# Nine input-projection blocks computed as seven block products during the first three attentions

## The reference

```python
proj = h @ w_in[layer]
(glu_a, glu_b, z_conv, q, k, v, z_att, g_conv, g_att) = jnp.split(proj, split_idx, axis=-1)
u = glu_a * jax.nn.sigmoid(glu_b)          # then a causal depthwise convolution of 31 taps
...                                         # silu(z_att) and sigmoid(g_conv), sigmoid(g_att) are used later
```

## Time and profile before

| | us |
|---|---|
| median of 3 runs (2577.93 to 2579.3) | 2578.81 |
| span of the profiled execution, first to last instruction | 2576.3 |
| TensorE busy | 2498.0 (97%) |
| VectorE busy | 1552.8 (60%) |
| ScalarE busy | 851.8 (33%) |
| GpSimd busy | 671.9 (26%) |
| attention stages 0, 1, 2 (from the first filler matmul to the next stage's first) | 191.9, 186.5, 172.8 |
| q, k, v stages 1 and 2 | 146.6, 144.9 |

### The profile page before, as it was taken

How to read it: one execution, slowest core, us unless ns; L and a number is a source line. 1 busy time by engine, 2 the same in 40 slices (tenths; PEclk the granted TensorE clock), 3 DMA queues, 4 the chain that set the end, 5 groups by cost and what they waited for, 6 DMA issues and landing times.

```text
span 2576.3 us, 31390 instructions
## 1 busy us (share of the span) xinstructions
PE 2498.0 (97%) x12016; PEld 2052.6 (80%) x12016; DVE 1552.8 (60%) x2476; ACT 851.8 (33%) x1664; POOL 671.9 (26%) x653
## 2 busy tenths in 40 slices
PE   7999999999999999989999999999999999999997
PEld 4787887887888887778888888887887788887875
DVE  7511348888778686565646521123557866858788
ACT  5213221122311222463114133231145545354453
POOL 3422223333234232322533332223310000000000
PEclk9999999999999999999999999999999999999998
DMA  7311212213231232633444122215449675666754
GB/s 254 103 49 46 71 64 61 71 42 99 83 92 50 71 101 77 220 105 128 131 137 136 31 86 73 74 66 176 140 118 294 132 196 146 167 192 164 196 126 104
DMA packets 163322, 300.83 MB, mean 117 GB/s; under 512 B 22114, under 2 KB 46434, under 8 KB 159332
## 3 DMA queue, kind: packets, MB, share of 16 engines
q1 hardware_dynamic: 143252, 250.05, 29.4%
q0 software_dynamic: 18768, 44.57, 9.6%
q10 hardware_dynamic: 1152, 4.19, 0.4%
HBM read 232.50 MB, written 57.87 MB: 113 GB/s over the span
## 4 chain that ended last, share of the span: by engine, by line
PE 79%; DVE 13%; DMA 3%; ACT 2%; issue 2%; POOL 1%; SPq 0%; DVEq 0%; ACTq 0%; POOLq 0%
PE ps L2302 51%; PE ps L2528 19%; DVE scr L1658 5%; PE ps L2426 3%; PE ps L2402 2%; PE ps L2412 2%; PE ps L2331 1%; DVE w_lo L2042 1%; DMA late_hi<-in_w_ada 1%; DMA h2c_d<-late_hi 1%; DVE w_lo L2051 1%; DVE big L2100 1%; DVE scr L1638 0%; POOL w_lo L1077 0%; DVE big L1898 0%
## 5 line engine op out<-in xcount | busy, mean ns | idle before, releaser
L2302 PE MATMUL ps<-act_hi,w_hi 128*128 128x512 f32 x1344 | 539.9, 402 | 13.3 <-DVE act_lo L1537 4.1
L2302 PE MATMUL ps<-act_lo,w_hi 128*128 128x512 f32 x1344 | 534.8, 398 | 0.0
L1075 POOL CAST w_hi<-raw 128x512 fp32r<-128x512 f32 x288 | 213.8, 742 | 1226.3 <-DMA raw<-in_w_in 757.3
L2302 PE MATMUL ps<-act_hi,w_lo 128*128 128x512 f32 x1344 | 526.9, 392 | 0.0
L1658 DVE SCALAR_TENSOR_TENSOR scr<-scr,small 128x512 f32<-128x512 f32 x480 | 433.0, 902 | 15.6
L1077 POOL TENSOR_TENSOR w_lo<-raw,w_hi 128x512 fp32r<-128x512 f32 x288 | 402.4, 1397 | 23.1
L2302 PE MATMUL ps<-w_hi,act_hi 128*128 128x512 f32 (+1 forms) x960 | 377.0, 393 | 3.9 <-POOL w_lo L1077 2.4
L2302 PE MATMUL ps<-w_hi,act_lo 128*128 128x512 f32 (+1 forms) x960 | 370.1, 386 | 0.0
L2302 PE MATMUL ps<-w_lo,act_hi 128*128 128x512 f32 (+1 forms) x960 | 369.4, 385 | 0.0
L2528 PE MATMUL ps<-w_hi 128*128 128x512 f32 x896 | 350.7, 391 | 10.7 <-issue 7.5
L2528 PE MATMUL ps<-w_lo,w_hi 128*128 128x512 f32 x896 | 349.3, 390 | 0.0
(11 more groups left out here) (235 smaller groups left out, 2674.5 us busy)
## 6 DMA issues: line engine op xcount, KB each, us to landing
raw<-in_w_in SPq DMA_DIRECT2D x176, 256.0 KB, 3.3
late_hi<-h2c_d SPq DMA_DIRECT2D x21, 1024.0 KB, 7.6
vreg<-in_w_ada SPq DMA_DIRECT2D x36, 256.0 KB, 5.4
raw<-in_w_in SPq DMA_DIRECT2D x72, 128.0 KB, 2.3
raw<-in_w_up POOLq DMA_DIRECT2D x8, 1024.0 KB, 11.6
late_lo<-in_w_up SPq DMA_DIRECT2D x8, 1024.0 KB, 5.5
late_lo<-in_w_up POOLq DMA_DIRECT2D x8, 1024.0 KB, 15.8
late_lo<-late_lo POOLq DMA_DIRECT2D x8, 1024.0 KB, 7.3
```

What stands on the lines that cost most here:

```text
L1075: pool.tensor_copy(dhi, src).then_inc(w_hi_done, 1)
L2302: ins = nc.tensor.matmul(out_, lhs, rhs, start=(m == 0), stop=(m == 3 * nk - 1))
```

## The change

Each of the nine 512-column filler chunks X·W (1024 x 1024 by 1024 x 512) is computed as a 2 x 2 by 2 x 2 block product in Winograd's form of Strassen: seven products of 512 x 512 by 512 x 256 operands in place of eight. A product is 2 tiles of 12 matmuls, so a block has 14 tiles of 12 matmuls: 1512 filler matmuls in all in place of 1728 (504 a stage in place of 576).

- Weights: a block has four quarters of 512 x 256, loaded by five DMAs of 512 KB (the third buffer is loaded three times) into three buffers (`raw` and a new `raw_c`). GpSimd forms four sums of 128 x 1024 elements and splits seven weight operands of 128 x 1024, each as two copies and two subtractions of 128 x 512 (`block_split`, `block_sum`, `block_weights`), into a ring of four operands. It starts on a stage's blocks when TensorE has done the last k unit before it.
- Activations: at the start VectorE forms four sums of 128 x 2048 elements between `h_lo` and the rotation's angles. Five quarters of 1 MB (four sums and A21) are stored to DRAM; ScalarE may not overwrite `big` before they are stored. In each attention stage nine forms of 1 MB are loaded again; ScalarE copies the high part (128 x 2048) and VectorE subtracts the low part (128 x 2048). They share chunk buffer 0 of the weights.
- Results: of the seven products of a tile ScalarE copies three from PSUM to SBUF and VectorE adds or subtracts three more banks to those in SBUF; the banks carry on accumulating between products. Tanh and gating follow on SBUF or PSUM.
- Two evacuation waits at the head of an attention stage move behind its first filler.
- The plan of the convolution's taps stays as it is.

```diff
+MULS = (12, 12, 12, 24)
+FILL = (504, 504, 504, 768)
+BLOCK_ORDER = (1, 2, 6, 5, 7, 3, 4)
+T_ORDER = (1, 2, 5, 6, 3, 7, 4)
+T_RING = 4
+BLOCK_KIND = ("glu", "glu", "glu", "glu", "gate", "gate", "gate", "gate", "silu")
+FORM_AT = (1, 3, 5, 7, 14, 21, 28, 35, 40)
...
+            def block_split(n, p, src):                      # GpSimd
+                j, slot_ = 7 * n + T_ORDER.index(p), ring_of(n, p)
+                if j >= T_RING:
+                    wait_block(pool, (j - T_RING) // 7, T_ORDER[(j - T_RING) % 7], 1)
+                for k in range(2):
+                    two = slice(2 * k, 2 * k + 2)
+                    hi, lo = t_ring[0][slot_][:, two, :], t_ring[1][slot_][:, two, :]
+                    pool.tensor_copy(hi, src[:, two, :]).then_inc(t_hi, 1)
+                    pool.wait_ge(t_hi, 2 * j + k + 1)
+                    pool.tensor_tensor(lo, src[:, two, :], hi.bitcast(F32), ALU.subtract).then_inc(t_split, 1)
+            def block_sum(n, i, dst, other):                 # GpSimd, four in a block
+                pool.wait_ge(t_split, 14 * n + (4, 6, 8, 12)[i])
...
+                pool.tensor_tensor(dst, dst, other, ALU.add).then_inc(t_sum, 1)
...
+            def form_load(g, i):                             # SyncE
...
+                sp.dma_start(form_part(place, 1).bitcast(F32),
+                             form_d[FORM_DRAM[name]].rearrange("p (k n) -> p k n", k=4)).then_inc(form_ld[place], 16)
+            def form_hi_of(g, i):                            # ScalarE, behind filler tile FORM_AT[i]
...
+                nc.scalar.activation(form_part(place, 0), form_part(place, 1).bitcast(F32), ACT.Copy
+                                     ).then_inc(form_hi, 1)
+            def form_lo_of(g, i):                            # VectorE, behind filler tile FORM_AT[i]
...
+                dve.wait_ge(form_hi, FORM_HI0 + form_count(g, i))
+                nc.vector.tensor_tensor(lo, lo.bitcast(F32), form_part(place, 0).bitcast(F32), ALU.subtract
+                                        ).then_inc(form_lo, 1)
+            def block_unit_out(g, i):                        # VectorE
+                n, p, t = block_unit(g, i)
+                if i >= 2:
+                    block_final(*block_unit(g, i - 2))
...
+                if p == 2:
+                    x = block_slot(n, "p", t)
+                    wait_bank_read(dve, n, 1, t)
+                    wait_block(dve, n, p, t)
+                    nc.vector.tensor_tensor(x, x, block_bank(n, p, t), ALU.add).then_inc(bank_signal(p, t), 1)
...
+            dve.wait_ge(lo_done, KT)                         # VectorE at the start
+            nc.vector.tensor_tensor(a22, a21, a22, ALU.subtract).then_inc(form_ready, 1)
+            dve.wait_ge(a21_st, A21_ST0 + 16)
...
-    nc = bacc.Bacc("TRN2", target_bir_lowering=False, num_devices=1)
+    nc = bacc.Bacc("TRN2", target_bir_lowering=False, num_devices=1, dynamic_dma_scratch_size=4096)
```

More of the change, by code:

```diff
@@ L108, in stored @@
         chunk((name, j), us)
[L110 to L116, removed]
+    for g in range(NG):
+        qkv(g, "qkv")
     gates = [("zc", t, 1) for t in range(8)] + [("zc", t, 0) for t in range(8)]
@@ L388, in build @@
         out_add = sem("out_add")
-        wq_ld = [sem(f"wq_ld{i}") for i in range(4)]
+        wq_ld = raw_ld
         ring_ld, h2_kept, h2_st = [sem("ring_ld0"), sem("ring_ld1")], sem("h2_kept"), sem("h2_st")
@@ new lines, in build @@
+        store_number, stored_before, slot_total = {}, {}, [0] * 6
+        for n, kind in enumerate(BLOCK_KIND):
+            for i, p in enumerate(BLOCK_ORDER):
+                for t in range(2):
+                    stored_before[(n, p, t)] = list(slot_total)
+                    for q, name in STORES[kind]:
+                        if q == p:
+                            s_ = block_slot_number(n, name, t)
+                            slot_total[s_] += 1
+                            store_number[(n, p, t)] = (s_, slot_total[s_])
+            if n % 3 == 2:
+                stored_before[("stage", n // 3)] = list(slot_total)
@@ new lines, in wait_block_stored, with wait_slot_stored, wait_stage_stored @@
+        def wait_block_stored(eng, n, p, t):
+            s_, count_ = store_number[(n, p, t)]
+            eng.wait_ge(block_st[s_], BLOCK_ST0[s_] + 16 * count_)
+        def wait_slot_stored(eng, n, p, t, name):
+            s_ = block_slot_number(n, name, t)
+            if stored_before[(n, p, t)][s_]:
+                eng.wait_ge(block_st[s_], BLOCK_ST0[s_] + 16 * stored_before[(n, p, t)][s_])
+        def wait_stage_stored(eng, g):
+            for s_ in range(6):
+                eng.wait_ge(block_st[s_], BLOCK_ST0[s_] + 16 * stored_before[("stage", g)][s_])
@@ new lines, in build, with form_part, form_loads @@
+        FORM_PLACE = {"s2": E_SLOT, "s4": E_SLOT, "s1": F_SLOT, "s3": A_SLOT, "a21": A_SLOT}
+        FORM_SEQ = ("s2", "s1", "s3", "s4", "s2", "s4", "s2", "s4", "a21")
+        FORM_DRAM = {"s1": 0, "s2": 1, "s3": 2, "s4": 3, "a21": 4}
+        def form_part(place, part):
+            if place == A_SLOT:
+                return (act_hi, act_lo)[part][:, 0:4, HALF:S]
+            k0 = 4 if place == E_SLOT else 0
+            return (w_hi, w_lo)[part][:, 0, k0:k0 + 4, :]
+        def form_loads(g, i):
+            place = FORM_PLACE[FORM_SEQ[i]]
+            per = sum(1 for x in FORM_SEQ if FORM_PLACE[x] == place)
+            return g * per + sum(1 for x in FORM_SEQ[:i + 1] if FORM_PLACE[x] == place)
@@ L836, in _ @@
             sp.wait_ge(stat_st, 16 * 4)
-            for t in range(4):
-                for h in range(2):
-                    wait_stored(sp, ("za", t, h))
+            wait_stage_stored(sp, NG - 1)
             for g in range(NG):
@@ L2265, in begin @@
                     pe.wait_ge(free_of(u), U[u] // ACC)
+                for g, first in enumerate(AFTER_QKV):
+                    if U[u] - first in range(ACC):
+                        j = U[u] - first
+                        wait_bank_read(pe, 3 * g + 2, 3 if j < 2 else 4, j % 2)
             def proj(u, m):
```

530 lines of the change are left out of this document (426 added, 104 removed).

## The result

The changed kernel takes 2749.58 us (median; 2744.68 to 2753.2) where the kernel before took 2578.37 us in the same comparison: a ratio of 1.0663, 95% interval 1.0651 to 1.0676, or +171 us. The forecast of 2686 us had the direction and the place, but the time lies 64 us above it, 5 us above the range of 8 in 10 (2595 to 2745) and 4 us above the range that the prediction's own sum gives (2651 to 2746).

The account below looks back on a forecast made before the run. TensorE bounds the kernel before; VectorE was to bound stages 1 and 2 after. Stage 1 +54.9, stage 2 +50.7, stage 0 -10, start +8, q, k, v +4 make +107.6: 2686 us, range of 8 in 10 2595 to 2745.

Parts of the forecast that it names:

- the interference of one split: Stages 1 and 2: one GpSimd split of 128 x 512 costs VectorE 1.13 us during an operation with two SBUF inputs.
- the descriptor space: Feed-forward part: the smaller space could only slow accumulating DMAs, of which few are open at a time; 0.
- Rival A: Whole kernel: TensorE keeps the path and the change is faster, 2535 us; chance 8%.
- B: Stages 1 and 2: GpSimd's added work falls mostly where VectorE is idle or reads PSUM; 2609 us, chance 13%.
- D: Attention stages: TensorE waits for weight operands or forms that come late; 2589 us, chance 4%.
- C: Stages 1 and 2: GpSimd's copies block VectorE too, interference 78 and 81 us; 2743 us, chance 7%.
- The waits w: Stages 1 and 2: VectorE's further waits, mainly for ScalarE's high parts before low parts; 15 us a stage, bounds 0 and 40.
- the interference x: VectorE's time lost to GpSimd in taps, low parts and SBUF gatings: 50.2 us in stage 1, 51.7 in stage 2.
- stage 0: First attention stage: TensorE stays the bound, VectorE at 138 of 175 us; -10 us, bounds -17 and -2.
- q, k, v (+4): Stages of q, k, v: more GpSimd units and a tail of the stage before; +4 us for both, 0 to 10.
- the rest: What follows stage 2: the feed-forward part stays as long as before, 0 us.
- VectorE over 85% busy: Sign in the profile after: VectorE's busy share in stages 1 and 2, with idle time before low parts put down to ScalarE.

Follow-up runs that it names:

- e1: Changed kernel with activation forms loaded in both parts and not split by ScalarE and VectorE, values not the reference's: 2665.7 us.
- e3: Changed kernel with GpSimd's subtractions and sums replaced by copies of one operand, values not the reference's: 2688.3 us.
- e4: Changed kernel with convolution taps, all but the first of a tile, on 256 of their 512 columns: 2675.5 us.
- e5: Changed kernel with ten more matmuls ahead of each step's transposes in stages 1 and 2, results equal: 2747.8 us.
- e7: Kernel before with only the form splits, nine a stage into an unread buffer, and the smaller descriptor space added: 2623.8 us.
- e10: Changed kernel with forms loaded unsplit, GpSimd's subtractions and sums as copies, and weight pieces loaded two tiles earlier; values not the reference's: 2596.87 us.
- e6: Changed kernel with the next chunk's first four weight pieces issued two filler tiles earlier, results equal: 2740.6 us.

## Why the prediction was wrong

Where it was right: VectorE takes over as the pacer of stages 1 and 2 (e1, e3, e4 shorten them, e5 does not lengthen them), the place and the size of TensorE's idle time (69 and 58 us, some 60 forecast), the interference of one split (1.13 forecast, 1.14 in single taps), the start (+8; +7.2), and the descriptor space (e7). Rival A is refuted by those 69 and 58 us, where it allowed 10, and by e5; B by the taps' 1.03 and 1.07 us and by e3; D inside the stages, where TensorE waits for no operand. C gave 2743 us, nearest to the time, but not by its mechanism: it wanted an interference of 78 us in stage 1, and e3 took away 32; a copy costs 0.23, not 0.61. GpSimd's subtractions did not stay near 1.3 us (1.62); that sign was misread from the start, as the earlier trace rows have 35.00 / 23 = 1.52 before the change.

The step that failed is **"The waits w"**, all the time in which VectorE stands still other than for the accumulator's store (small gaps included): I took 15 us of a range of 0 to 40, arguing that VectorE waits then for scores anyway. It was 60.4 us in stage 1 and 50.7 in stage 2, above even the upper bound, and VectorE waits for scores only 1.7 us. For stage 1 the forecast was 164.3 us of work, 11.9 for the accumulator's store, 15 of waits, 50.2 of interference, 241.4 together. Measured are 192.2 us busy, so 27.9 of interference, and 69.9 us idle: 38.2 for ScalarE's high parts, 9.5 for the stores, 15.4 for banks of products to add (L2111 to L2121), 1.7 for scores, and the rest in small gaps. That is 43 us more idle time and 22 less interference, +20.7 in sum. For stage 2: 175.7 busy in place of 201.3, 57.9 idle in place of 22.2, +10.1. I had put the six waits between scores and transposes at 18 us, and then discounted them to 15 with all others; eight waits measured 38, and the additions' waits had no number of their own. e1 shows that about half of the low parts' waits is on the path (18.5 of 38.2 us, 15.0 of 29.5). How much of the additions' waits is, no run shows; e10's remaining 8 us in stage 1 only leave room for it.

The second term, **the interference x**, was too large, by 22 us in stage 1 and 26 in stage 2. It made up for 22 of the 43 us by which the waits were off in stage 1, and 26 of 36 in stage 2: that the stages came out only 21 and 10 us off is partly luck. The unit price held, and the number of units nearly: 62 were forecast; stage 1 has 34 subtractions, 9 double sums and 6 of the next pieces' splits, 58, and stage 2 has 53. But I applied the loss to the low parts as well, and these were hardly slower (21.99 us for nine, 21.9 forecast), and in a stage that waits lengthen, less of the time is two-input work (156 of 262 us in stage 1, taps, low parts and gatings). What was lost is in the taps: 131.6 less 128 x 0.76, and 119.3 less 112 x 0.76, 34 us in each stage (rows of single lines overlap a little, so they don't add up to the 27.9).

Third, **stage 0** was put at -10 and gave -1.5. VectorE was busy 104.3 us there, not the 138 of the forecast, and TensorE still stood still for 10 us. e1, e3 and e4 shorten the stage by 5.6, 2.8 and 2.8 us, and with e1, e3 and e6 together it is the -10.3 of e10; so the loss goes back to the splits and the lengthened taps in single steps, which my comparison of VectorE's sum with the whole stage hid. Which steps they are was not looked at.

Fourth, **q, k, v (+4) and "the rest" (0)** gave +20.2 and +12.8. The step on D said that SyncE's order puts a form's load behind a store that waits for taps, and dismissed it since GpSimd keeps up. It looked at the blocks' operands only, and not at the next chunk's pieces, which are in the same queue. e6 gave back 9 us in all, 7.8 and 3.9 of them in these stretches. By the counts of matmuls the late pieces could account for most of the 33; how much of it they do, and what else is in it, was not tried.

The sum of the misses: 20.7 + 10.1 + 8.5 + 16.2 + 12.8 - 0.8 = 67.5 us, against 2751.4 - 2683.9 = 67.5 for the spans (forecast span 2576.3 + 107.6).

"VectorE over 85% busy" was a wrong sign to look for: an engine that paces with waits in its loop is 73% busy here, and TensorE, which doesn't pace, 74%. What told them apart was an experiment that adds work to one (e5) and one that removes it from the other (e4).

## What to carry to other kernels

When work is moved from the pacing engine to others, count it on each engine step by step, against the spare time of that step, and give every cross-engine handshake that the new work brings a number of its own when it stands ahead of something that the loop needs. Two operands of one split made on two engines cost VectorE 22 us of work and 38 of waits in a stage, and 40 us came back without them; store what is split once and load it in both parts if the DMA has room. When a queue in program order gets new transfers, look at each transfer behind it that a later stage's first instruction needs.

## What the runs showed of the hardware

- A tap of 0.76 us takes 1.67 beside GpSimd's subtraction of 128 x 512, 0.99 beside its copy, and 2.72 beside its sum of 128 x 1024; the copy goes from 0.61 to 1.07. The Trainium skill ("SBUF — State Buffer", Who interferes with whom) says that the one that comes second is blocked for the whole instruction and that issue order decides who it is. The rows agree: GpSimd's instruction and the tap take turns, each waiting for the rest of the other, and a blocked tap's time is about the other's remaining time plus its own.
- A long instruction loses little in such a meeting, against its length. VectorE's low parts of 128 x 2048, also with two SBUF inputs, take 2.28 us with nothing beside them. In stages 1 and 2 they took 2.28 to 3.29: at most 1.0 more, where they began inside a subtraction of GpSimd. Subtractions that began inside a low part took 3.2 to 3.4 us in place of 1.28, and sums 4.3 in place of 2.4. In all, nine low parts lost 1.5 us in stage 1 and 2.3 in stage 2, and the taps 34 in each.
- TensorE's granted clock fell to a mean of 0.86 in stages 1 and 2 with 26 and 25% of the time idle, and to 0.59 in the 20 us after stage 0, where the pieces came late (the first matmul of a piece takes 0.79 us there in place of 0.47). Raising it to 0.92 did not shorten the stages (e5).
